# Input stage of a hybrid encoder layer: other PSUM banks for odd value blocks, convolution taps ahead of the next gated block, and the state product behind two states

## What is computed

```python
z = x @ w_in                       # columns: conv value | conv gate | q | k | v | g | low-rank forget
# group A, 1024 channels
u = a * sigmoid(gate)
y = depthwise_causal_conv(u, width 31) + conv_b
y = silu(layer_norm(y))            # over the 1024 channels
# group B, 4 heads, dk = 128, dv = 256, chunks of 64 rows
log_a = log_sigmoid(f_lr @ gate_w + gate_b) / 16
S_t = diag(a_t) S_{t-1} + k_t^T v_t ;  o_t = q_t S_t
o = o * rsqrt(mean(o * o)) * norm_g * silu(g)
x = layer_norm(alpha * x + concat(y, o) @ w_out)
```

## Time and profile before

| | us |
|---|---|
| median of three runs (3616.63 to 3646.29) | 3618.85 |
| the profiled execution | 3619.7 |
| its span, first to last instruction | 3617.9 |
| PE busy (97% of the span) | 3507.1 |
| DVE busy (76%) | 2749.4 |
| POOL busy (51%) | 1855.6 |
| ACT busy (33%) | 1187.6 |

### The profile page before, as it was taken

One profiled execution on the slowest core, in us unless ns is written; L12 is line 12 of the kernel. 1 busy time (PEld: TensorE's weight loads), 2 busy tenths in 40 slices (PEclk: granted clock), 3 DMA queues, 4 the chain that ended last, 5 costly groups with the idle time before them and its releaser, 6 DMA issues. The chain is left out here.

```text
span 3617.9 us, 62512 instructions
## 1 busy us (share of the span) xinstructions
PE 3507.1 (97%) x25292; PEld 3462.4 (96%) x25292; DVE 2749.4 (76%) x3474; ACT 1187.6 (33%) x1152; POOL 1855.6 (51%) x1107
## 2 busy tenths in 40 slices
PE   8999999798999999999999999999999999999996
PEld 7999999797999999999999999999999999999996
DVE  4866859734799887777777777776688888888877
ACT  2332333322322234444444344443222222222223
POOL 3434433354544477877877780001666666665321
PEclk9999999899999999999999999999999999999998
DMA  3222222355215678888888887777799999899962
GB/s 144 82 76 77 81 72 71 137 220 216 101 70 175 188 205 230 226 228 218 227 227 224 226 226 228 217 230 283 276 356 350 356 356 360 343 361 353 356 247 96
DMA packets 466251, 788.22 MB, mean 218 GB/s; under 512 B 78976, under 2 KB 376384, under 8 KB 402384
## 3 DMA queue, kind: packets, MB, share of 16 engines
q1 hardware_dynamic: 337920, 547.99, 46.1%
q0 software_dynamic: 83840, 168.15, 14.6%
q10 hardware_dynamic: 44368, 70.57, 5.3%
HBM read 711.43 MB, written 209.34 MB: 255 GB/s over the span
## 5 line engine op out<-in xcount | busy, mean ns | idle before, releaser
L609 POOL TENSOR_TENSOR wl<-wraw,wh 128x512 fp32r<-128x512 f32 x352 | 534.4, 1549 | 695.4 <-ACT wh L1071 687.5
L660 POOL DMA_INDIRECT g_scratch<-picks,g_col x384 | 683.5, 1780 | 174.8 <-issue 148.5
L1071 ACT ACTIVATE wh<-wraw 128x2048 fp32r<-128x2048 f32 x216 | 414.1, 1918 | 977.8 <-PE ps L989 741.6
L989 PE MATMUL ps<-Wh,wh 128*128 128x384 f32 x2048 | 687.2, 336 | 6.7 <-DVE wl L1949 3.9
L989 PE MATMUL ps<-Wl,wh 128*128 128x384 f32 x2048 | 685.9, 335 | 0.0
L989 PE MATMUL ps<-Wh,wl 128*128 128x384 f32 x2048 | 685.8, 335 | 0.0
L708 PE MATMUL ps<-xh,wh 128*128 128x272 f32 x2304 | 490.0, 294 | 29.7 <-POOL xl L632 13.0
L957 PE MATMUL ps<-xh,wl 128*128 128x272 f32 x1792 | 518.5, 289 | 0.0
L957 PE MATMUL ps<-xl,wh 128*128 128x272 f32 x1792 | 515.5, 288 | 0.0
L957 PE MATMUL ps<-xh,wh 128*128 128x272 f32 x1792 | 515.2, 287 | 0.3 <-DVE wl L1834 0.3
L708 PE MATMUL ps<-xh,wl 128*128 128x272 f32 x2304 | 480.6, 290 | 0.0
(11 more groups left out here) (299 smaller groups left out, 7011.5 us busy)
## 6 DMA issues: line engine op xcount, KB each, us to landing
wraw<-in_u_t SPq DMA_DIRECT2D x128, 1024.0 KB
v_rows<-in_v_t SPq DMA_DIRECT2D x256, 512.0 KB
wraw<-in_v_t SPq DMA_DIRECT2D x128, 1024.0 KB
wraw<-in_w_in SPq DMA_DIRECT2D x40, 1024.0 KB
g_scratch<-zeros ACTq DMA_DIRECT2D x32, 768.0 KB, 4.6
h_scratch<-hb ACTq DMA_DIRECT2D x64, 384.0 KB
gt<-g_scratch SPq DMA_DIRECT2D x64, 384.0 KB
hg<-h_scratch SPq DMA_DIRECT2D x64, 384.0 KB
```

Of the source, the lines that this page charges most:

```text
L609: ins = nc.gpsimd.tensor_tensor(wl[:, u, part], wraw[:, u, part], f(wh[:, u, part]), ALU.subtract)
L660: nc.gpsimd.indirect_dma_start(g_elem, bass.IndirectOffsetOnAxis(ap=idx, axis=0), gate, None, compute_op=ALU.add).then_inc(g_put, 16)
L989: ins = mat(out, w[:, u, d * EG + e], m[:, e], start=(begin and e == 0 and w is wh and m is Wh[v]), stop=(end and e == EG - 1 and w is wl))
L1071: go(wh[:, u], wraw[:, u], ACT.Copy).then_inc(whi, 1)
```

## The change

The values of odd convolution blocks (except the last, block 7) and the last head's q now go to banks 6 and 7 instead of 0 and 1, so that the jobs that write them need not wait for the `glu` of the block before. The wait of a head's q job is for `glu(2h)`, where it was for `glu(2h + 1)`. On VectorE all 31 taps of block 2h stand ahead of `glu(2h + 1)`; within a head the taps of the other block are moved two places back; `glu(7)` stands after tap 26 instead of after tap 30 of block 6. PE's sample product waits for a new count `p_first`, which goes up after the second of the eight states, instead of for the eighth.

```diff
+        def value_ps(c):
+            return yr(1) if c % 2 and c < CT - 1 else zr(0)
+
+        def q_ps(h):
+            return yr(1) if h == LAST else zr(0)
...
             def conv_waits(c, gate):
...
                 if c % 2:
-                    return [(sg_s if gate else glu_s, c)]
+                    return [(sg_s, c)] if gate else []
                 return [(z_out, 3 * c if gate else 3 * c - 1)] if c else []
...
             def head_job(h, j, **part):
-                if h == LAST and j not in (2, 3):
-                    w = [((glu_s, sg_s)[j % 2], CT - 1 if j < 2 else CT)]
+                if j == 0:
+                    w = [] if h == LAST else [(glu_s, 2 * h + 1)]
+                elif j == 1:
+                    w = [(sg_s, CT - 1 if h == LAST else 2 * h + 2)]
+                elif h == LAST and j == 2:
+                    w = [(glu_s, CT - 1)]
+                elif h == LAST and j >= 4:
+                    w = [((glu_s, sg_s)[j % 2], CT)]
                 else:
-                    w = [(z_out, 6 * h + j - 1)] if j >= 2 else [((glu_s, sg_s)[j], 2 * h + 2)]
-                job(j % 2, n_head(h, j), xh, xl, zr(j % 2), w, **part)
+                    w = [(z_out, 6 * h + j - 1)]
+                job(j % 2, n_head(h, j), xh, xl, zr(j % 2) if j else q_ps(h), w, **part)
...
-                pe.wait_ge(p_out, 2 * h + 1)
+                pe.wait_ge(p_first, h + 1)
                 mat(ps[:, 4, 0:DV], kdN[0:TS, NC], vN[0:TS, NC], start=True, stop=True).then_inc(p_mm, 1)
...
                 distances(0)
-                conv_taps(c1, 4, 6)
                 for l in range(6):
                     if l < 5:
                         distances(l + 1)
-                    conv_taps(c1, 6 + 2 * l, 8 + 2 * l)
+                    if l:
+                        conv_taps(c1, 4 + 2 * l, 6 + 2 * l)
...
                     C.done(tt_(ke[l % 2][:, 0:n], k[:, 0:n], dist[l % 2][:, 0:n], ALU.mult), qke)
+                    if l == 0:
+                        conv_taps(c1, 4, 6)
...
-                conv_taps(c1, 24, CW)
+                conv_taps(c1, 22, 27)
                 if h == LAST:
                     glu(CT - 1)
+                conv_taps(c1, 27, CW)
                 conv_end(c1)
...
                                 ps[:, 4 + c // 2, (c % 2) * DV:(c % 2 + 1) * DV], ALU.mult, ALU.add),
-                           p_out if c == NC - 1 else dve)
+                           p_out if c == NC - 1 else p_first if c == 1 else dve)
...
                 if h < LAST:
                     conv_rows(2 * h)
-                    conv_taps(2 * h, 0, CW // 2)
+                    conv_taps(2 * h, 0, CW)
+                    conv_end(2 * h)
                     glu(2 * h + 1)
-                    conv_taps(2 * h, CW // 2, CW)
-                    conv_end(2 * h)
                 gla(h)
```

## The result

The changed kernel takes 3642.13 us (median of 10 runs, 3638.95 to 3674.52), the kernel before 3619.88 on the same chip (10 runs, 3615.63 to 3649.07): a recorded ratio of 1.0083 [1.0054, 1.0111] (the two medians alone give 1.0061). It is slower, by 22 us between the medians. That is less than the one per cent that counts as a difference here, but the interval of the ratio leaves 1 out. The forecast was 3605, the range ended at 3637: the prediction was wrong, and the time came out near that of rival 2 (3645).

A forecast was written before the change was run, and what follows sets the result against it. PE, busy for 97% of the span, was taken as the bound. Waits 18.2 us plus clock 3.4, last head -1.0, gave 20.6 less; minus 7 for late POOL, 13.6 less: 3605 us, range 3594 to 3637.

The forecast's parts named there:

- rival 2: POOL's first group is kept out of VectorE's taps, PE idles before q jobs in heads 0 to 2; 3645 us, chance 0.28.
- The step that failed: Head 1: POOL's first operation, arriving 0.27 us into a VectorE tap, was taken as let in, between 0.13 and 0.58.
- one second group late for 7 us: POOL's operations for the k job's weights, late in head 1 or 2: 5.6 us idle PE plus 1.7 us clock.
- rival 1: POOL always gets in after one VectorE tap, as the skill page's rule gives; 3598 us, chance 0.33.
- the row of 6.48 us: Head 1, kernel before: one POOL operation for the q job's tile took 6.48 us, elsewhere 1.3 to 1.8.
- The waits for `ext`: PE's waits for gated blocks in heads 0 to 2 go: part of 10.8 us booked.
- The clock: Half clock behind two PE waits, at block 1 and head 0's q job, goes: 3.4 us less.
- The last head: VectorE is the engine the border waits for, so PE's gains come back as later waits: loss of 1.0 us (0 to 3).
- Rival 3: VectorE binds the scores: late gated blocks delay decays, `ke` waits grow, 8 to 9 us lost; 3607 us, chance 0.05.

The follow-up runs named there:

- the sixth experiment: The changed kernel with a single pause (VectorE waits for its own tap) behind tap 4 of the run of 31; 3624.6 us, ratio 1.0026.
- the quarters: The changed kernel with each tap of the long run cut into four pieces and one pause behind tap 0; 3674.7 us, run once.

## Why the prediction was wrong

**The step that failed** is the reading of when POOL is let in: "0.27 us into the tap of 224.75. ... I take it as let in, since it is nearer to the first". Two things were wrong in it. The moment was off (it came 0.04 us into a tap in heads 1 and 2, 0.21 in head 0), and the moment does not matter. The earlier trace rows had three arrivals, and I read the wrong quantity off them. The one at 238.63 came in the second tap after `glu`'s break and was let in; the one at 226.06 came in the eighth instruction of an unbroken run, and that at 252.75 in the fifteenth. An arrival 1.04 us sooner than 226.06 falls one tap earlier, in the seventh instruction, and the edge lies between the sixth and the seventh: in heads 1 and 2 the changed kernel missed it by one instruction. What it showed in place of "let in" is an operation of 19.35 us and 14.1 us of idle PE in each. Head 0 had no term in the forecast at all: there POOL came in the twelfth instruction, was held for 15.53 us, and PE idled for 10.27.

**The conclusion drawn from it**, one second group late for 7 us, therefore never came up in the changed kernel; its mechanism is right, as the sixth experiment shows. There the second groups were kept out and PE idled 5.31 us, where I had put 5.6.

**The Trainium skill's rule** (SBUF — State Buffer, Who interferes with whom: the second to issue is blocked until the first finishes) holds for arrivals in the first six instructions, in operations of 1.3 to 1.9 us. Beyond them the runs contradict it: 19.35 us, and 31.82 in the quarters. I had weighed it as rival 1 at 0.33 and had the row of 6.48 us against it.

**The steps that held.** Rival 2's price: 14.6 us of idle PE in heads 1 and 2 against 14.08 and 14.09, 13 us with the clock in head 0 against 10.27 + 3.0, and 47 us in all against 46.7. POOL was kept out in all three heads, and the time was slower than before, as its sign said. The reason that rival 2 gave, 0.27 us into a tap being too late, did not come true: in heads 1 and 2 POOL came 0.04 us into the tap, and the sixth experiment let it in at 0.57 us. So the price was read rightly, and that the condition held was luck. The waits for `ext`, for `ke` (4.5 to 0.9) and for the states in heads 0 to 2 went as booked. The gated block 3 came at 253.3 us instead of 236.9, and that cost PE nothing: its waits for `ext` came to 0.2 us in all.

**Sizes that were off.** The clock: rival 2 had 1.7 to 2.8 us behind a stall and it was 2.4 to 3.0. The last head: I booked a loss of 1.0 us and it gained 2.3 (147.7 us from the head mean of head 2 to the output projection before, 145.4 after). The gaps of 1.04 and 1.10 us and a stretch of 3.4 us at half the clock went from it. I had taken VectorE's chain for the bound of this head. Then PE's gain would have come back as a longer wait at the border, and that wait was 15.5 us against 15.1.

**The chances.** Rival 3 was given 0.05 as a case of its own. Longer waits for `ke` showed in each of the four kernels with short waits for `wl` (6.8 to 12.0 us, against 4.5 before the change), in one of them with the gated block in its old place. So with POOL let in the time is 3602.5 us and not the 3598 of rival 1.

## What to carry to other kernels

When a reordering makes one engine's run of instructions unbroken, ask who else needs SBUF during it, and count the instructions between the points at which that engine stands, not the microseconds. A wait for its own last result costs that engine 0.2 us (0.91 from tap to tap instead of 0.73) and lets the neighbour in; with one behind every eighth tap this kernel is at 3602.5 us, below the kernel before (3617.1) and the changed one (3642.1). And before a term decides a forecast, list every instance of the event in the trace and ask which quantities go together in it. In the kernel before, the arrivals with at least two taps to come lay in the first or second instruction of a run and at most 0.34 us into that instruction, or in the eighth and at least 0.56 us into it. That trace could not tell a place in a tap from a place in a run; it took kernels that move the one and leave the other.

## What the runs showed of the hardware

- POOL's TENSOR_TENSOR with two SBUF inputs that starts in the seventh instruction or later of a run of VectorE's taps, each with two SBUF inputs and none waiting for the last, is held until the run ends: up to 31.82 us. In the first six it is let in after the tap at hand. Taps 0 and 1, TENSOR_SCALAR with one SBUF tensor as input, count in the run.
- Once in, operation and tap take turns to the end of POOL's group: with full taps four operations in 6.6 to 7.0 us, a tap 1.8 us instead of 0.73.
- Why it is six stays open, and the sixth itself rests on one arrival; so does whether other instructions of VectorE or other sizes of POOL's operation move the edge. The two arrivals of 3.02 us say that the rule is not complete.
- Behind stalls of 10.27 to 14.09 us PE worked for another 4.7 to 6.0 us at half the clock (1.2 GHz).
- Halves and quarters cost VectorE more than their share: a quarter takes 0.285 us against 0.73 for a whole tap, which makes the run 1.56 times as long.
